# Three exact fp32 sums of squares per mixer step become pairs of rounded products, with the low parts on GpSimd

## The reference

```python
q = _rms_norm(q.reshape(b, s, ATTN_HEADS, 2, ATTN_HEAD_DIM), q_g, RMS_EPS) * (ATTN_HEAD_DIM ** -0.5)
k = _rms_norm(k.reshape(b, s, ATTN_HEADS, 2, ATTN_HEAD_DIM), k_g, RMS_EPS)
...
o = _rms_norm(o, sub_g, RMS_EPS) * (1.0 - lambda_init)
```

## Time and profile before

| What | Value |
|---|---|
| Median of 3 runs | 1875.05 us (1873.26 to 1875.48) |
| The profiled execution's own time | 1873.98 us |
| Its span, first to last instruction | 1871.9 us |
| PE busy | 1828.2 us, 98% of the span |
| DVE, ACT, POOL busy | 1130.2, 941.7, 355.5 us |
| Granted PE clock | 0.999 of full speed |

### The profile page before, as it was taken

The page is one execution under the profiler, slowest core; times in us unless marked ns, Lnnn a source line. Parts: engine busy times, 40 slices in busy tenths (PEclk is TensorE's granted clock), DMA queues, the critical chain, the costliest instruction groups (busy, mean ns, idle before and its releaser), DMA issues.

```text
span 1871.9 us, 27360 instructions
## 1 busy us (share of the span) xinstructions
PE 1828.2 (98%) x8657; PEld 1297.2 (69%) x8657; DVE 1130.2 (60%) x1373; ACT 941.7 (50%) x1310; POOL 355.5 (19%) x401
## 2 busy tenths in 40 slices
PE   8999999999999999999999999999999999999997
PEld 6887887887887888887655665566556655565553
DVE  7767867867867333448664565456545654565456
ACT  5676676666667222325454455445544554455441
POOL 0322332332330000013011112111211121112010
PEclk9999999999999999999999999999999999999999
DMA  6232232232241222458999999999999999999998
GB/s 203 86 122 94 81 132 92 79 129 100 79 138 57 92 100 97 161 195 320 419 419 421 421 422 421 422 421 422 421 421 421 421 421 421 421 422 421 422 421 333
DMA packets 95377, 520.06 MB, mean 278 GB/s; under 512 B 13522, under 2 KB 20858, under 8 KB 45032
## 3 DMA queue, kind: packets, MB, share of 16 engines
q1 hardware_dynamic: 87672, 501.08, 67.0%
q0 software_dynamic: 6944, 16.30, 2.3%
q10 hardware_dynamic: 720, 2.16, 0.3%
HBM read 511.52 MB, written 25.51 MB: 287 GB/s over the span
## 4 chain that ended last, share of the span: by engine, by line
PE 77%; DMA 12%; DVE 6%; issue 2%; ACT 2%; SPq 0%; DVEq 0%; ACTq 0%
PE bank L1919 18%; PE bank L1300 15%; PE bank L1682 10%; DMA big<-in_w 9%; PE bank L1330 7%; PE bank L1950 7%; PE bank L1959 6%; DVE w_lo L2514 2%; PE bank L1375 2%; PE bank L1942 1%; PE bank L1358 1%; DVE x_lo L2526 1%; PE bank L1442 1%; PE bank L1862 1%; ACT w_hi L2206 1%
## 5 line engine op out<-in xcount | busy, mean ns | idle before, releaser
L2514 DVE TENSOR_TENSOR w_lo<-big,w_hi 128x2048 fp32r<-128x2048 f32 x141 | 322.1, 2293 | 204.1 <-ACT w_hi L2206 204.1
L2206 ACT ACTIVATE w_hi<-big 128x2048 fp32r<-128x2048 f32 x141 | 268.7, 1917 | 229.0 <-DMA big<-in_w 204.6
L1950 PE MATMUL bank<-big,keep 128*64 128x512 f32 x896 | 203.3, 598 | 0.0
L2514 DVE TENSOR_TENSOR w_lo<-keep,w_hi 128x2048 fp32r<-128x2048 f32 x48 | 109.9, 2292 | 105.0 <-ACT w_hi L2206 104.0
L1300 PE MATMUL bank<-h_hi,wm_hi 128*128 128x512 f32 x408 | 168.7, 414 | 0.0
L1300 PE MATMUL bank<-h_hi,wm_lo 128*128 128x512 f32 x408 | 159.6, 391 | 0.0
L1300 PE MATMUL bank<-h_lo,wm_hi 128*128 128x512 f32 x408 | 159.0, 390 | 0.0
L2206 ACT ACTIVATE w_hi<-keep 128x2048 fp32r<-128x2048 f32 x48 | 92.2, 1921 | 106.6 <-DMA keep<-in_w 97.8
L1950 PEld LDWEIGHTS bank<-big,keep 128*64 128x64 f32 x896 | 59.9, 136 | 117.3 <-issue 117.2
L1919 PE MATMUL bank<-w_hi,x_hi 128*128 128x512 f32 x480 | 134.5, 402 | 2.9 <-DVE w_lo L2514 2.7
L1919 PE MATMUL bank<-w_lo,x_hi 128*128 128x512 f32 x480 | 129.0, 390 | 0.0
(11 more groups left out here) (398 smaller groups left out, 3619.5 us busy)
## 6 DMA issues: line engine op xcount, KB each, us to landing
big<-in_w SPq DMA_DIRECT2D x290, 1024.0 KB, 13.0
keep<-in_w SPq DMA_DIRECT2D x94, 1024.0 KB, 14.7
big<-in_w_mix SPq DMA_DIRECT2D x72, 512.0 KB, 3.3
keep<-in_w_tail SPq DMA_DIRECT2D x44, 512.0 KB, 3.3
keep<-in_x SPq DMA_DIRECT2D x8, 512.0 KB, 4.6
aux<-acum_rows SPq DMA_DIRECT2D x16, 256.0 KB, 3.8
big<-acum_rows SPq DMA_DIRECT2D x16, 256.0 KB, 3.7
keep<-y_tok SPq DMA_DIRECT2D x4, 1024.0 KB, 14.4
```

What stands on the lines that cost most here:

```text
L1950: ins = pe.matmul(bank[2 * (c // 2)][r, :], x_s[:, n % 4, CS * (n // 4):CS * (n // 4 + 1)], raw[s][:, c * 512:(c + 1) * 512], start=False, ...
L2206: act.activation(w_hi[:, s], raw[r], ACT.Copy).then_inc(hi_ready, 1)
L2514: dve.tensor_tensor(w_lo[:, s], raw[r], w_hi[:, s].bitcast(F32), ALU.subtract).then_inc(lo_ready, 1)
```

## The change

For each of the three squares a high part `sq_hi` is made on ACT, in the rounded format, and a low part `sq_lo` (square minus high part, written over the square) on GpSimd. PE multiplies the rounded ones matrix by each of them and adds in the same bank. `sq_hi` lies where the attention logits lie (`L`). GpSimd's program of a step is put in another order and its last step is written out; two rounded constants are made once on GpSimd before its loop. Three semaphores of the overflow branch of the experts are shared with others, to free numbers.

```diff
+        block_r, ones_r = parts("block_r", [P, P], big_base, loop_mem.at + 4 * D), sb("ones_r", [P, 1], F32R)
+        sq_hi, sq_lo = parts("sq_hi", [P, 2, T], aux_base, 0), parts("sq_lo", [P, 2, T], keep_base, 23552 - 3 * KT * P)
...
+                def low_square(i, n, at):
+
+                    pool.wait_ge(sqhi_ready.sem, sqhi_ready.at(i, at))
+                    pool.tensor_tensor(sq_lo[:, n], sq[:, n], sq_hi[:, n].bitcast(F32), ALU.subtract).then_inc(
+                        sqlo_ready.sem, 1)
+
+                def body(i, more):
+                    make_seg(i, 1)
+                    make_xs(i, 0)
+                    low_square(i, 0, 1)
+                    low_square(i, 1, 2)
+                    make_seg(i, 2)
+                    make_xs(i, 1)
+                    make_seg(i, 3)
+                    make_xs(i, 2)
+                    make_xs(i, 3)
+                    if more:
+                        make_seg(i + 1, 0)
+                    low_square(i, 0, 3)
+
+                make_seg(0, 0)
+                pool.tensor_copy(block_r[:], block_ones)
+                pool.tensor_copy(ones_r[:], ones[:, 0:1])
+                steps_of_mixer(pool, body)
...
                         act.activation(sq[:, n], proj_b[n][:], ACT.Square).then_inc(proj_read.sem, 1)
+                        act.wait_ge(proj_read.sem, proj_read.at(i, n + 1))
+                        act.wait_ge(diff_ready.sem, diff_ready.at(i, 0))
+                        act.activation(sq_hi[:, n], sq[:, n], ACT.Copy).then_inc(sqhi_ready.sem, 1)
...
                     act.activation(sq[:, 0], m1_b[:], ACT.Square).then_inc(osq_ready.sem, 1)
+                    act.wait_ge(osq_ready.sem, osq_ready.at(i, 1))
+                    act.activation(sq_hi[:, 0], sq[:, 0], ACT.Copy).then_inc(sqhi_ready.sem, 1)
...
-                        pe.matmul(s_b[n][:], block_ones, sq[:, n], start=True, stop=True).then_inc(sums_ready.sem, 1)
+                        pe.wait_ge(sqlo_ready.sem, sqlo_ready.at(i, n + 1))
+                        pe.matmul(s_b[n][:], block_r[:], sq_hi[:, n], start=True, stop=False)
+                        pe.matmul(s_b[n][:], block_r[:], sq_lo[:, n], start=False, stop=True).then_inc(
+                            sums_ready.sem, 1)
...
-                    pe.matmul(s_b[0][:], ones, sq[:, 0], start=True, stop=True).then_inc(osum_ready.sem, 1)
+                    pe.wait_ge(sqlo_ready.sem, sqlo_ready.at(i, 3))
+                    pe.matmul(s_b[0][:], ones_r[:].to_broadcast([P, P]), sq_hi[:, 0], start=True, stop=False)
+                    pe.matmul(s_b[0][:], ones_r[:].to_broadcast([P, P]), sq_lo[:, 0], start=False, stop=True).then_inc(
+                        osum_ready.sem, 1)
```

More of the change, by code:

```diff
@@ L409, in decoder_layer @@
                                                            sem("halves_ready"))
-        ovhot_ready, ovhot_used, ovtable_ready, over_ready = (sem("ovhot_ready"), sem("ovhot_used"),
+        ovhot_ready, ovhot_used, ovtable_ready, over_ready = (Again(hot_ready, NT), Again(hot_used, NT - 1),
                                                               sem("ovtable_ready"), sem("over_ready"))
+        sqhi_ready, sqlo_ready = sig("sqhi_ready", 3), sig("sqlo_ready", 3)
         raw_in = [sem(f"raw_in{n}") for n in range(RAW)]
@@ L633, in _ @@
             def _(pool):
-                prime(pool, seg_ready, xs_ready, gidx_ready, sidx_ready, pickb_ready, picks_ready, *spare_used[0:2])
+                prime(pool, seg_ready, sqlo_ready, xs_ready, gidx_ready, sidx_ready, pickb_ready, picks_ready, *spare_used[0:2])
                 pool.wait_ge(decays_ready, 3)
[L636 to L672, removed]
@@ new lines, in heads, with make_seg @@
+                def heads(table, i, u):
+                    return table[:, u, bass.ds(i * HPG, HPG)]
+                def make_seg(i, u):
+                    pool.wait_ge(rows_in[u % 2].sem, rows_in[u % 2].at(i, u // 2 + 1))
+                    of = seg_of[u % 2].rearrange("p k (h c) -> p k h c", h=2)
+                    at = heads(a_all, i, u).rearrange("p (k h) -> p k h", k=2)
+                    pool.tensor_tensor(of, of, at.unsqueeze(3).to_broadcast([P, 2, 2, P]), ALU.subtract).then_inc(
+                        seg_ready.sem, 1)
+                    pool.wait_ge(seg_ready.sem, seg_ready.at(i, 2 * u + 1))
+                    pool.tensor_tensor(of, of, tri.unsqueeze(1).unsqueeze(1).to_broadcast([P, 2, 2, P]), ALU.mult).then_inc(
+                        seg_ready.sem, 1)
@@ new lines, in make_xs @@
+                def make_xs(i, u):
+                    pool.wait_ge(m0_read.sem, m0_read.at(i, u + 1))
+                    pool.wait_ge(m1_ready.sem, m1_ready.at(i, min(2 * u, 6)))
+                    pool.wait_ge(ydiag_ready.sem, ydiag_ready.at(i, u))
+                    pool.wait_ge(y_read.sem, y_read.at(i, u))
+                    xv = xb[:, u, 0:GW].rearrange("p (h c) -> p h c", h=HPG)
+                    for dst, src in ((xdt, heads(dtv, i, u)), (xw, heads(wend, i, u))):
+                        pool.tensor_tensor(dst.rearrange("p (h c) -> p h c", h=HPG), xv,
+                                           bcast_inner(src, HD), ALU.mult)
+                    dsk = SMALL["d_skip"][0]
+                    pool.tensor_tensor(xd.rearrange("p (h c) -> p h c", h=HPG), xv,
+                                       bcast_inner(smalls[:, bass.ds(i * HPG + dsk, HPG)], HD),
+                                       ALU.mult).then_inc(xs_ready.sem, 1)
@@ L674, in _ @@
+                make_seg(0, 0)
+                pool.tensor_copy(block_r[:], block_ones)
+                pool.tensor_copy(ones_r[:], ones[:, 0:1])
+                steps_of_mixer(pool, body)
             @block.scalar
             def _(act):
-                prime(act, sigz_ready, phi_ready, ghi_ready, sigm_ready, mhi_ready, taps_ready, silu_ready, proj_read, root_ready, m0_read, decay_ready, exp_ready, yn_ready,
+                prime(act, sigz_ready, sqhi_ready, phi_ready, ghi_ready, sigm_ready, mhi_ready, taps_ready, silu_ready, proj_read, root_ready, m0_read, decay_ready, exp_ready, yn_ready,
@@ L2090, in head_ov @@
                     for t in range(NT):
-                        pe.wait_ge(ovhot_ready, t + 1)
+                        pe.wait_ge(ovhot_ready.sem, ovhot_ready.at(t + 1))
                         for k in range(TOPK):
@@ L2094, in head_ov @@
                                             start=(t == 0 and k == 0), stop=(t == NT - 1 and k == TOPK - 1))
-                        ins.then_inc(ovhot_used if t < NT - 1 else ovtable_ready, 1)
+                        ins.then_inc(ovhot_used.sem if t < NT - 1 else ovtable_ready, 1)
                 overflow(pe, head_ov, body_ov)
@@ L2735, in head_ov @@
                         if t:
-                            dve.wait_ge(ovhot_used, t)
+                            dve.wait_ge(ovhot_used.sem, ovhot_used.at(t))
                         dve.tensor_tensor(ov_hot, bcast_mid(slot_no, TOPK), bcast_inner(posx[:, n], CAP), ALU.is_equal)
@@ L2740, in head_ov @@
                         dve.tensor_tensor(ovid_hot, ovid_hot, bcast_inner(entry1[:, n], NOV + 1), ALU.mult).then_inc(
-                            ovhot_ready, 1)
+                            ovhot_ready.sem, 1)
                     dve.wait_ge(ovtable_ready, 1)
```

## The result

The changed kernel takes 1912.43 us (median of 4 runs, 1911.2 to 1916.4), the kernel before 1875.26; the ratio is 1.0208, with a 95% interval of 1.0196 to 1.0219. It is slower by about 37 to 39 us, where I had forecast 24 and a range up to 1907. The profiled execution has a span of 1909.5 us, 37.6 more than before.

A forecast was written before the change was run, and what follows sets the result against it. PE, busy for all of a mixer step, was taken to set the pace. Three sums, 2.84 - 0.39 + 0.55 = 3.00 us a step, 24.0 us in eight, gave 1898.5 us, range 1887 to 1907.

The forecast's parts named there:

- The first sum's term: At `sum_squares(0)` PE stops 3.2 us for the low part; less the faster products, 2.84 us lost a step.
- Rival 1: The port lock between DVE and GpSimd does not bite at the first sum: 1887 to 1890 us, chance 0.10.
- queue of three: GpSimd's low part queues behind `make_xs(0)` while DVE waits for the shared ports; DVE goes first, else 1.2 us less a step.
- rival 3: PE's stop of 3.2 us brings the clock to its lower level in the mixer: 13 us more, 1911, chance 0.05.
- Its price: Lower clock level lasting as long as PE's stop, half of that lost: 1.6 us a step, 13 in all.
- The third sum: PE waits for the low part on GpSimd, begun 0.38 us after ACT's end: 0.55 us lost a step.
- The second sum: PE comes after `project_vz(0)`, finds both parts ready and does not wait: 0.39 us gained a step.
- What is taken from PE's sequence is gained: PE, busy all 68.69 us of a mixer step, sets the pace, so its savings and waits reach the kernel's end unchanged.
- rival 2: The operands are there in time and 24 sums save 0.40 us each, 9.6 us: about 1865 us, chance 0.03.
- What hid the rest: Idle time covers the later `make_seg(1)`, GpSimd's 2.4 us and the constants; without it each costs under 1 us once.

The follow-up runs named there:

- run 2: The changed kernel with 6 extra rounded products on PE ahead of its wait for the first low part: 1899.74 us, ratio 1.0131.
- run 1: The changed kernel with 13 extra rounded products on PE ahead of its wait for the first low part: 1895.59 us, ratio 1.0117.
- Run 6: The kernel before with only the third sum as a rounded pair, in its old place: 1876.95 us, ratio 1.0017.
- runs 4 and 5: 4: changed kernel without low parts, second products reading the high part again, 1872.1 us; 5: kernel before with only the second sum as a pair, 1873.53 us.
- run 11: All three sums as pairs; q and k low parts on DVE, `sum_squares(0)` behind transposes 2, third sum one eighth project later: 1869.66 us, ratio 0.9977.

## Why the prediction was wrong

- **The direction and the mechanism of the stop were right.** The first sum's term was 2.84 us; in an undisturbed step the transposes and `y_and_state(0)` stand 351.10 - 346.98 = 4.12 us apart, before 123.04 - 121.85 = 1.19, so 2.93. The low part, which no row of before showed, took the 1.30 us taken for it, and DVE had the turn. Rival 1 (the lock doesn't bite) is out. The rule of the Trainium skill, "SBUF — State Buffer", "Who interferes with whom", that the one that issues first holds the ports for its whole instruction, gave the right answer for the queue of three: 2.24 us against 1.30 alone, since DVE, which was waiting, went first.
- **The step that failed is the way in which rival 3, the clock, was handled.** The prediction gave it a chance of 0.05 and ended its range at 1907, below the 1911 that it had itself worked out for this case. Its only ground was that the clock stayed at 1.00 in the experts, where PE is idle for 22 us of 900; but there the idle time comes in pieces of 1.8 us at most, and the new stop of 3 us was longer than any that PE had behind its first product. And one trace without a fall was thin ground even for 1.8 us: other traces show falls behind the very same stop (run 2). It should have been the likely case and stood in the sum, which it would have raised to 24 + 13 = 37 us. That this is nearly the 37.6 us of the profile is in part luck: the waits cost 22 and not 24, the clock 17 and not 13.
  The Trainium skill, "TensorE: Matmul & The Clock Gate", "Part 1: The HAM clock gate", says that an idle PE is throttled to half speed; the trace agrees in six steps, 1.00 to 0.50 at the end of the stop, and in the other two the clock stayed at 1.00 behind the same stop.
- **Its price** was set as low level for as long as the stop, 1.6 us a step. It lasted up to twice as long, but not in each step: 34.1 us in all, 17 us of loss by run 1, where I had 13.
- **The third sum** was put at +0.55. GpSimd began 0.08 us after ACT's end (110.95 to 111.03), not 0.38, and from the last transposes to the next project PE took 1.43 us (111.52 to 112.95) and not 1.08, 0.35 more. Run 6 gives 0.4.
- **The second sum**: -0.39 on PE, but nothing for the kernel when no long stop stands ahead of it (runs 4 and 5). "What is taken from PE's sequence is gained" was read from a PE that is busy for all of the step. A busy share of 100% shows that PE waits for nothing, not that nothing else stands right behind it. Even with all in place, the 9.6 us of rival 2 were not to be had: the best version found has 4.3.
- **What hid the rest** held: `make_seg(1)` behind the third low part, the constants, and ACT's copy of the second square cost nothing that a wait shows.

Open: why the clock fell in some steps and not in others at equal stops, how much of the differences under 2 us between runs is its chance falls behind the mixer, and whether more of the 9.6 us can be had by relieving DVE between `norm_qk(0)` and `gate_y(2)`, or by moving `take_y(0)` ahead of `norm_y(2)` in ACT's order: its transposes began at 162.12 in the kernel before, and ACT sat idle for the 1.39 us up to 163.53. None of these was tried.

## What to carry to other kernels

When a change makes the busiest engine wait, work out the stop first, and then ask what the clock does behind it: a stop of 3 us on PE cost two thirds as much again as it lasted (17 us for eight of 3.05). A saturated engine may have two other engines within 0.3 us of it; look at how late the operands of each group really are before counting a saving on it in full. And where an operand is late, moving the question (one line of the consumer's order, 28 us here) can be worth nearly as much as making it on a freer engine (34 us), and run 11 takes both.

## What the runs showed of the hardware

The granted clock fell after stops of 3.05 us in 6 of 8 steps, of 2.0 us in 6 of 8, of 1.7 us in 2 of 8, of 0.94 and 0.23 us close together in 1 of 8 (one profiled execution each), each time for 3 to 7 us. Of the 13 traces, 5 show a fall behind the last stop of 1.76 us, and 7 show one between 842 and 871 us where PE had no idle time in the 4 us before, but a run of products of 32 columns (in run 11 at 842.2 us). So an idle stop isn't the only thing ahead of a fall, and a single trace doesn't tell whether a place is safe. GpSimd writes the rounded format at no extra cost (1.30 us for 128x512, as line 650 with 1.29). A first rounded product behind a wait takes 0.34 us to the second (350.52 to 350.86) and not 0.23; its load of weights starts with it, at 350.52, where the second's starts 0.23 us ahead (350.63). In run 11, where no idle time of PE stands ahead of the third pair, it still takes 0.30 us (106.94 to 107.24), with the load at 106.91.
